# Prompt attention with two kv heads as a pair on TensorE's array

## The reference

```
s = einsum('...qhgd,...khd->...hgqk', q, k) * (HEAD_DIM ** -0.5)
s = where(mask, s, NEG_INF)            # a block of 128 queries sees its own and the previous 128 keys
m = maximum(max(s, axis=-1), sink)     # sink: one learned logit for each head
p = exp(s - m)
denom = sum(p, axis=-1) + exp(sink - m)
o = einsum('...hgqk,...khd->...qhgd', p / denom, v)
```

## Time and profile before

| | |
|---|---|
| median of three runs | 1669.94 us (1668.59 to 1674.22) |
| span of the profiled execution, first to last instruction | 1674.7 us; the page gives no other time of its own for it |
| prompt attention, first scores to first matmul of the output projection | 1127.39 to 1218.83 us |
| TensorE busy over the span | 1625.3 us, 97% |
| mean granted clock of TensorE over the span | 0.974 |

### The profile page before, as it was taken

One profiled execution on the slowest core, in us unless ns is written; L12 is line 12 of the kernel. 1 busy time (PEld: TensorE's weight loads), 2 busy tenths in 40 slices (PEclk: granted clock), 3 DMA queues, 4 the chain that ended last, 5 costly groups with the idle time before them and its releaser, 6 DMA issues.

```text
span 1674.7 us, 27448 instructions
## 1 busy us (share of the span) xinstructions
PE 1625.3 (97%) x11258; PEld 1487.3 (89%) x11258; DVE 853.0 (51%) x1042; ACT 535.7 (32%) x829; POOL 154.8 (9%) x147
## 2 busy tenths in 40 slices
PE   7999999999999899999999999989999999999997
PEld 7689879969977799999999999955599999999997
DVE  6457338437635764334434476456656443443343
ACT  4243144225324332212222252136823221222221
POOL 0010001001000330000000040222322000000001
PEclk9999999999999999999999999975999999999999
DMA  6246217226324342222222232200022322232223
GB/s 232 83 158 214 78 63 243 90 69 207 121 63 140 112 153 96 81 93 83 88 88 88 88 101 63 64 8 1 1 68 86 100 87 89 75 100 81 96 76 104
DMA packets 49683, 164.48 MB, mean 98 GB/s; under 512 B 5665, under 2 KB 5729, under 8 KB 49569
## 3 DMA queue, kind: packets, MB, share of 16 engines
q1 hardware_dynamic: 41472, 134.23, 25.2%
q0 software_dynamic: 7408, 26.78, 4.3%
q10 hardware_dynamic: 720, 2.26, 0.3%
HBM read 141.82 MB, written 23.46 MB: 99 GB/s over the span
## 4 chain that ended last, share of the span: by engine, by line
PE 87%; DVE 6%; ACT 3%; issue 2%; DMA 1%; POOL 0%; ACTq 0%; DVEq 0%; SPq 0%; POOLq 0%
PE ps L358 65%; PE ps L372 8%; PE ps L864 2%; PE ps L1138 2%; PE ps L858 2%; DVE arena L1180 2%; PE ps L1160 2%; PE ps L846 1%; PE ps L1149 1%; DVE s_lo L1180 1%; PE ps L876 1%; DVE xg_lo L1186 1%; DVE arena L1278 1%; PE ps L1052 1%; PE ps L1099 1%
## 5 line engine op out<-in xcount | busy, mean ns | idle before, releaser
L358 PE MATMUL ps<-xg_hi,w_hi 128*128 128x272 f32 x1728 | 360.1, 290 | 11.5 <-DVE xg_lo L1186 8.2
L358 PE MATMUL ps<-xg_hi,w_lo 128*128 128x272 f32 x1728 | 358.0, 289 | 0.0
L358 PE MATMUL ps<-xg_lo,w_hi 128*128 128x272 f32 x1728 | 356.8, 288 | 0.0
L341 ACT ACTIVATE w_hi<-w_raw 128x1024 fp32r<-128x1024 f32 x220 | 227.2, 1052 | 374.3 <-PE ps L358 218.4
L346 DVE TENSOR_TENSOR w_lo<-w_raw,w_hi 128x1024 fp32r<-128x1024 f32 x220 | 281.6, 1297 | 63.3 <-ACT w_hi L341 57.7
L358 PE MATMUL ps<-pr_hi,w_hi 128*128 128x272 f32 x1440 | 304.4, 291 | 7.3 <-DVE pr_lo L1180 3.9
L358 PE MATMUL ps<-pr_hi,w_lo 128*128 128x272 f32 x1440 | 301.3, 289 | 0.0
L358 PE MATMUL ps<-pr_lo,w_hi 128*128 128x272 f32 x1440 | 300.3, 288 | 0.0
L358 PEld LDWEIGHTS ps<-xg_hi,w_hi 128*128 128x128 f32 x1728 | 273.3, 189 | 20.8 <-DVE w_lo L346 7.7
L358 PEld LDWEIGHTS ps<-xg_lo,w_hi 128*128 128x128 f32 x1728 | 272.0, 189 | 0.0
L358 PEld LDWEIGHTS ps<-xg_hi,w_lo 128*128 128x128 f32 x1728 | 270.3, 189 | 0.0
(11 more groups left out here) (202 smaller groups left out, 1459.3 us busy)
## 6 DMA issues: line engine op xcount, KB each, us to landing
w_raw<-in_w SPq DMA_DIRECT2D x220, 512.0 KB, 3.6
arena<-in_state SPq DMA_DIRECT2D x32, 512.0 KB, 4.5
out_st_s<-arena POOLq DMA_DIRECT2D x32, 512.0 KB, 4.7
x<-in_x ACTq DMA_DIRECT2D x4, 544.0 KB, 5.8
out_y<-x POOLq DMA_DIRECT2D x8, 272.0 KB, 2.3
out_st_p<-arena SPq DMA_DIRECT2D x4, 512.0 KB, 2.8
arena<-in_dec POOLq DMA_DIRECT2D x4, 256.0 KB, 3.0
arena<-in_cache_v POOLq DMA_DIRECT2D x1, 1024.0 KB, 8.7
```

The source lines that it names most:

```text
L341: nc.scalar.activation(w_hi[:, n.c % 4, :], w_raw[:, n.c % 2, :], ACT.Copy).then_inc(w_hi_done, 1)
L358: last = pe.matmul(ps[:, 2 * bank_pair + s, 0:HT], w_of(w, k), xm[:, k, s * HT:(s + 1) * HT], start=(k == 0 and w == 0 and xi == 0), stop= ...
```

## The change

Units 2m and 2m+1 have the same block c and neighbouring kv heads, one on each half of the array. `scores`, and `values`, of TensorE now take such a pair m. Inside `scores(m)`, each query head is done for one half of the array's rows and then for the other; inside `values(m)`, each key block is done for columns 0 to 63 and then for columns 64 to 127. Both units of a pair share bank 6 or 7, by the parity of m, on different partitions. `turned` stays one unit at a time. There are four buffers for the turned probabilities in place of two. The orders of ScalarE, VectorE and GpSimd stay as they are.

```diff
-A_PS, A_PPT = (7808, 8832, 10880, 11904), (12960, 9856)
+A_PS, A_PPT = (7808, 8832, 10880, 11904), (12960, 9856, 6720, 13984)
...
             def probs_t(n):
                 k0 = 1 if units[n][0] == 0 else 0
                 act.wait_ge(att_tr, NKV + n + 1)
-                if n >= 2:
-                    act.wait_ge(att_pv, NKV + n - 1)
-                nc.scalar.activation(ar(A_PPT[n % 2], 2, 512)[:, k0:2, :], ps[:, 4 + k0:6, :], ACT.Copy).then_inc(att_pt, 1)
+                act.wait_ge(att_pv, NKV + max(n - 3, 0))
+                nc.scalar.activation(ar(A_PPT[n % 4], 2, 512)[:, k0:2, :], ps[:, 4 + k0:6, :], ACT.Copy).then_inc(att_pt, 1)
...
-            def scores(n):
-                c, g = units[n]
-                u, rows = g // 2, slice(64 * (g % 2), 64 * (g % 2) + 64)
+            def scores(m):
+                c, u = units[2 * m][0], units[2 * m][1] // 2
                 w0 = P if c == 0 else 0
-                pe.wait_ge(att_masked, NKV + max(n - 1, 0))
+                pe.wait_ge(att_masked, NKV + 2 * m)
                 for j in range(4):
-                    last = pe.matmul(ps[:, 2 * (n % 2) + j // 2, (j % 2) * 256 + w0:(j % 2) * 256 + 256], qt[rows, 4 * u + j, tok(c + 1)],
-                                     kt[rows, u, NS_TOK + P * (c - 1) + w0:NS_TOK + P * (c + 1)], start=True, stop=True)
-                last.then_inc(att_s, 1)
+                    for i in range(2):
+                        rows = slice(64 * i, 64 * i + 64)
+                        last = pe.matmul(ps[:, 2 * i + j // 2, (j % 2) * 256 + w0:(j % 2) * 256 + 256], qt[rows, 4 * u + j, tok(c + 1)],
+                                         kt[rows, u, NS_TOK + P * (c - 1) + w0:NS_TOK + P * (c + 1)], start=True, stop=True)
+                        if j == 3:
+                            last.then_inc(att_s, 1)
...
-            def values(n):
-                c, g = units[n]
-                rows = slice(64 * (g % 2), 64 * (g % 2) + 64)
+            def values(m):
+                c, u = units[2 * m][0], units[2 * m][1] // 2
                 k0 = 1 if c == 0 else 0
-                pe.wait_ge(att_pt, NKV + n + 1)
-                pe.wait_ge(att_lo, NKV + n - 1)
-                pt = ar(A_PPT[n % 2], 2, 512)
+                pe.wait_ge(att_pt, NKV + 2 * m + 2)
+                pe.wait_ge(att_lo, NKV + max(2 * m - 2, 0))
                 for kk in range(k0, 2):
-                    last = pe.matmul(ps[rows, 6 + n % 2, :], v_att[:, c + kk, g * HD:g * HD + HD], pt[:, kk, :], start=(kk == k0), stop=(kk == 1))
-                last.then_inc(att_pv, 1)
-
-            for n in range(-DEPTH, len(units)):
-                if n + DEPTH < len(units):
-                    scores(n + DEPTH)
-                if 0 <= n + 1 < len(units):
-                    turned(n + 1)
-                if n >= 0:
-                    values(n)
+                    for i in range(2):
+                        g, pt = 2 * u + i, ar(A_PPT[(2 * m + i) % 4], 2, 512)
+                        last = pe.matmul(ps[64 * i:64 * i + 64, 6 + m % 2, :], v_att[:, c + kk, g * HD:g * HD + HD], pt[:, kk, :],
+                                         start=(kk == k0), stop=(kk == 1))
+                        if kk == 1:
+                            last.then_inc(att_pv, 1)
+
+            pairs = len(units) // 2
+            for m in range(-2, pairs):
+                if m + 2 < pairs:
+                    scores(m + 2)
+                if 0 <= m + 1 < pairs:
+                    turned(2 * m + 2)
+                if m >= 0:
+                    values(m)
+                if 0 <= m + 1 < pairs:
+                    turned(2 * m + 3)
```

More of the change, by code:

```diff
@@ L782, in outs @@
                 nc.scalar.activation(xg_hi[lo_p:lo_p + 64, 4 * u:4 * u + 4, tok(c + 1)],
-                                     ps[lo_p:lo_p + 64, 6 + n % 2, :].rearrange("p (j t) -> p j t", j=4), ACT.Copy).then_inc(att_hi, 1)
+                                     ps[lo_p:lo_p + 64, 6 + (n // 2) % 2, :].rearrange("p (j t) -> p j t", j=4), ACT.Copy).then_inc(att_hi, 1)
             for n in range(-DEPTH, len(units)):
@@ L1576, in att_rest @@
                 dve.wait_ge(att_hi, NKV + n + 1)
-                tt(xg_lo[lo_p:lo_p + 64, 4 * u:4 * u + 4, tok(c + 1)], ps[lo_p:lo_p + 64, 6 + n % 2, :].rearrange("p (j t) -> p j t", j=4),
+                tt(xg_lo[lo_p:lo_p + 64, 4 * u:4 * u + 4, tok(c + 1)], ps[lo_p:lo_p + 64, 6 + (n // 2) % 2, :].rearrange("p (j t) -> p j t", j=4),
                    xg_hi[lo_p:lo_p + 64, 4 * u:4 * u + 4, tok(c + 1)].bitcast(F32), ALU.subtract).then_inc(att_lo, 1)
```

## The result

The changed kernel is slower: 1693.45 us median (1691.32 to 1694.67, 4 runs), against 1672.08 (1668.59 to 1678.16) for the kernel before measured beside it; the ratio of all runs is 1.0112 with a 95% interval of 1.0076 to 1.0149 (the medians divided give 1.0128). The forecast was 1685 us, in a range of 1673 to 1694; its own narrower range, 1680 to 1692, was missed by 1.5 us. In the profiled execution the span is 1691.9 us, 17.2 more than before, and the time of that execution is 1694.02 us, so 2.1 us lie outside the span.

The account below looks back on a forecast made before the run. The prediction took a closed loop of waits across TensorE, VectorE and ScalarE to bound prompt attention. Span 1674.7 + 12.7 = 1687.4, less 2 for the profiled execution's gap to the median, gave 1685 us, range 1673 to 1694.

Parts of the forecast that it names:

- a loop: Six waits in prompt attention from one pair's scores to the next: 10.7 us at 2.4 GHz, 13.4 at 1.2 GHz.
- Steps 2 and 3: VectorE's masking, maximum and negation before the exponentials, 3.15 us; then ScalarE's exponentials of unit 2m+4, 2.8 us.
- steps 4 and 5: ScalarE's outputs of unit 2m, 0.6 us, then its evacuation of the transposes of unit 2m+2, 1.17 us.
- The larger hole: TensorE idle behind a pair's values, waiting for ScalarE's next evacuation: 3.2 us a round at 2.4 GHz.
- The overlap: TensorE runs both array halves at once: a pair of score blocks 2.03 us, a pair of value blocks 2.1 us.
- Step 1: First score matmul of a pair to VectorE's masking, taken as the whole pair: 2.03 us, 1.8 more at 1.2 GHz.
- the halves do not overlap: Rival, 8%: no overlap on TensorE, scores 1.9 or 3.7 us longer in each of six rounds, total 1695 us.
- Two thirds of the work at the low level: TensorE's clock goes up and down each round or two; two thirds of the work at 1.2 GHz, +12.7 us.
- P(2): Start of the scores of pair 2 (other numbers likewise), put at 1140.0 us in the profile at 1.2 GHz.
- the tail: Work from the start of the last pair's scores, behind which nothing overlaps: 25.4 us, 7.4 more at 1.2 GHz.
- Full clock throughout: Rival, 17% together with the as-before clock: TensorE at 2.4 GHz throughout, span 1673.4 us, some 1671 against the median.
- ScalarE's throughput: Rival, 5%: ScalarE's own work bounds prompt attention, five rounds of 8.6 us, total 1663 us.

Follow-up runs that it names:

- the one-line edit on ScalarE: Changed kernel with one ScalarE line moved, so the exponentials come one unit later; 1675.3 us, ratio 1.0030 to the kernel before.
- filler: Changed kernel with three more float32 products of 512 columns, never read, behind each pair of values; 1683.38 us, ratio 1.0067 to the kernel before.
- The blocks kernel: Changed kernel with pair order kept but alternation taken out: one half's block, then the other's; 1688.89 us, ratio 1.0120 to the kernel before.
- the swapped one: The blocks kernel with the block of rows 64 to 127 first and VectorE waiting for both blocks; 1705.07 us, ratio 1.0195 to the kernel before.
- the reordered kernel with blocks: The reordered kernel with alternation taken out, one half's block and then the other's; 1671.87 us, ratio 0.9980 to the kernel before.
- the reordered kernel: Changed kernel with the queues of TensorE, ScalarE and VectorE reordered, scores one pair further ahead, same instructions; 1666.23 us, ratio 0.9961 to the kernel before.

## Why the prediction was right, and where it was off

*That the order forms a loop: right, and shown twice.* The waits name both legs, and the one-line edit on ScalarE takes 17 us out of the stage. Rounds were given as 10.7 us at the full level and 13.4 at the low one; measured, 10.52 (filler) and 13.2. Steps 2 and 3 are the same to 0.02 us (3.15 and 2.82), steps 4 and 5 together 1.53 in place of 1.77. The larger hole was put at 3.2 us; it is 4.3 to 5.5 in the changed kernel, where the values and transposes behind the evacuation run at the full level and the scores on the loop at the low one; with the filler, at the full level, it is the 3.2 that was given.

*The overlap: right.* A pair of score blocks takes 2.00 us at the full level (each of the last four of the filler kernel) and a pair of value blocks 1.94, against 2.03 and 2.1; nothing of the 2.5 us that the prediction weighed and left out of its sum is there. The proof from the earlier trace rows was weaker than it was put: the 4 and 9 matmuls are those under way in a stretch, not those that began in it, and all 16 took 1.71 us, 12 steps and not 8, since blocks in sequence overlap only in part.

*Step 1 was too wide.* "Scores to VectorE's masking" is one unit's block, not the pair's. Its length was right because an overlapped pair takes as long as one block. The rival "the halves do not overlap" was priced at 1.9 to 3.7 us more in each round, and that is too much, but not by far: in the alternated order the first unit's last matmul is the fourteenth of 16, so without overlap VectorE would start six steps later. By the difference of 8 and 12 steps (2.00 and 2.96 us at the full level, 3.79 and 5.65 at the low one) that is an estimated 1.4 to 2.8 us. No run is without overlap. The blocks kernel (1688.9) is not that case, since its order puts the first unit's block in front; the swapped one shows that a longer step 1 does lengthen the stage.

*The clock: right in kind, its size in part by luck.* Two thirds of the work at the low level gave +12.7 us for the stage; it was +12.2 (103.7 against 91.4, and the 91.4 is itself 3.4 us more than in two later executions). The low level covers half of the stage (mean clock 0.75), but its share of the score pairs, which are on the loop, is larger: the six steady ones took 3.77, 2.97, 3.60, 3.77, 3.77 and 2.69 us in the chain, where the full level would be 1.98. In the steady rounds the clock fell inside the holes of 4.3 to 5.5 us and rose while transposes and a pair of scores ran without a gap, as argued from the kernel before. With the hole filled, the clock stayed up for 54 us. But the length of one hole does not tell it. With the exponentials later the clock stayed up for 37.5 us over holes of 1.2 to 2.5 us, and in the reordered kernel with blocks it fell at 1176.7 us for 10.2 us, although no hole in the 17 us at the full level ahead of that was longer than 1.8. And the kernel before stood at the low level for 41 us without a hole for most of it. What decides is not shown by these runs.

*The sum by parts.* P(2) was put 12.6 us into the stage and came at 12.7; from there to P(7) 52.6 (full) to 65.7 (low) was worked out, 63.7 measured; the tail 25.4 to 32.8, 27.4 measured. With two thirds of the way to the low level that is 61.3 and 30.3: the rounds were put 2.4 us too short and the tail 2.9 us too long, and the two misses cancel in the +12.7.

*Why 1685 and not 1693.* The stage was sized right; the rest of the sum was not. I set the span equal to the time (2.1 us lie outside), took 2 us off for the profiled execution being at the top of the runs (here it was 0.6 above the median, so 1.4 too much), and left out the output projection at the low level, which I had seen but kept for the range (1.5 us behind the stage). 3.4 us more are ahead of the stage, in code that no edit touches; this start scatters from 1125.8 to 1130.8 us over the kernels here. The number alone, 1693.45, lies nearer to the rival "the halves do not overlap" (1695) than to the forecast; it is the rows, 3.79 us for 16 score matmuls at the low level and 2.00 at the full one, that rule it out.

*Full clock throughout* (17%): with the filler the clock was nearer to that (0.89 over the stage), and the kernel still 0.67% slower than before. That rival's time of 1673 rested on the whole stage at 2.4 GHz; in the change the hole stayed empty and the mean was 0.75. *ScalarE's throughput:* false for the change, true for the reordered kernel (its own figures, 9.6 us off the full-clock case, give 1663.8 us and not 1663). The Trainium skill (TensorEngine Tiling (Array Packing), "PSUM Bottleneck") says that the copy out of PSUM may become the bottleneck once TensorE is four times as fast. In the changed kernel it did not: ScalarE is idle for 29 us, waiting for maxima, while TensorE waits for ScalarE. In the reordered kernel the engine that copies is the bound, but of a round of 8.6 us only 3.0 are copies (L775, L781) and 5.4 are exponentials (L764, L767).

## What to carry to other kernels

When work is batched on one engine, write down the order on every other engine that takes part and follow one item round: if the evacuation that frees the next batch stands behind work on the batch just issued, all latencies add up, however fast the batched part has become. Check which half of the batch the loop really needs before pricing a faster pair. And a hole at TensorE can cost twice, once as idle time and once as the clock that the next blocks then run at: here, filling it with products that nobody reads took 8.8 us off the stage.

## What the runs showed of the hardware

Blocks for opposite halves of the array overlap without alternation in the program, but only in part: two score blocks of eight matmuls in sequence took 5.65 us at the low level, 12 steps. The first matmul of the second block started at 1190.36 us, together with the fifth of the first block and ahead of its last three, so between the halves the matmuls do not strictly keep the order in which they are written. With alternation all 16 take 8 steps (3.79 us).

The kernel before, unchanged, took 1660.6 to 1681.0 us in 25 runs, more than the 0.3% that I had taken as the limit of a measurement; the changed kernel stayed within 1691.3 to 1694.7 in four, and the reordered one within 1662.7 to 1668.5 in ten. The stage of the kernel before depends on when its clock rises, 31 or 41 us behind the fall in three traces, under the same instruction stream.
